# Down and output projections: the order of the three terms of a split product, high·high, low·high, high·low instead of high·high, high·low, low·high

## The reference

```python
x = x + mixer(rmsnorm(x, g1)) @ w_o            # output projection, 1024 x 1024
u = rmsnorm(x, g2) @ w_up                      # 1024 x 5632
g, v = split(causal_conv3(u))
x = x + (silu(g) * v) @ w_down                 # down projection, 2816 x 1024
```

## Time and profile before

| | us |
|---|---|
| median of 3 runs | 1048.58 |
| lowest, highest | 1048.35, 1048.67 |
| the profiled execution | 1048.49 |
| its span, first to last instruction | 1046.7 |
| TensorE matmul busy | 1041.2 |
| TensorE weight loads busy | 972.2 |
| VectorE, ScalarE, GpSimd busy | 866.1, 687.8, 348.1 |

### The profile page before, as it was taken

How to read it: one execution, slowest core, us unless ns; L and a number is a source line. 1 busy time by engine, 2 the same in 40 slices (tenths; PEclk the granted TensorE clock), 3 DMA queues, 4 the chain that set the end, 5 groups by cost and what they waited for, 6 DMA issues and landing times.

```text
span 1046.7 us, 21191 instructions
## 1 busy us (share of the span) xinstructions
PE 1041.2 (99%) x7496; PEld 972.2 (93%) x7496; DVE 866.1 (83%) x1589; ACT 687.8 (66%) x1264; POOL 348.1 (33%) x370
## 2 busy tenths in 40 slices
PE   9999999999999999999999999999999999999998
PEld 8999999999999999999989899999998998999998
DVE  7877778777799988887776999888896769998886
ACT  7766776766766656576776766655686766665662
POOL 5312222122355333322121564333350025543332
PEclk9999999999999999999999999999999999999999
DMA  9654555455466555535453666565434436665541
GB/s 321 226 162 152 159 159 171 147 174 203 160 217 212 196 195 188 173 107 181 144 180 121 202 210 208 184 191 192 145 107 144 152 119 215 213 198 192 190 157 41
DMA packets 57749, 183.34 MB, mean 175 GB/s; under 512 B 6352, under 2 KB 9680, under 8 KB 57424
## 3 DMA queue, kind: packets, MB, share of 16 engines
q1 hardware_dynamic: 56816, 181.52, 53.6%
q10 hardware_dynamic: 864, 0.92, 0.3%
HBM read 181.36 MB, written 1.05 MB: 174 GB/s over the span
## 4 chain that ended last, share of the span: by engine, by line
PE 94%; DVE 5%; DMA 0%; issue 0%; ACT 0%; DVEq 0%
PE ps L417 20%; PE ps L419 10%; PE ps L665 10%; PE ps L667 9%; PE ps L666 9%; PE ps L1747 6%; PE ps L1749 6%; PE ps L1748 6%; DVE w_lo L385 2%; PE ps L1223 2%; PE ps L1224 2%; PE ps L1225 2%; PE ps L599 1%; PE ps L843 1%; PE ps L888 1%; PE ps L817 1%
## 5 line engine op out<-in xcount | busy, mean ns | idle before, releaser
L385 DVE TENSOR_TENSOR w_lo<-w_raw,w_hi 128x1024 fp32r<-128x1024 f32 (+2 forms) x369 | 443.6, 1217 | 41.6 <-ACT w_hi L377 41.3
L377 ACT ACTIVATE w_hi<-w_raw 128x1024 fp32r<-128x1024 f32 (+2 forms) x369 | 353.8, 972 | 141.7 <-PE ps L419 119.0
L417 PE MATMUL ps<-xg,w_hi 128*128 128x512 f32 x1056 | 364.4, 391 | 0.0
L419 PE MATMUL ps<-xg,w_lo 128*128 128x256 f32 x1056 | 292.0, 277 | 0.0
L417 PEld LDWEIGHTS ps<-xg,w_hi 128*128 128x128 f32 x1056 | 198.3, 188 | 40.0 <-DVE xg L482 0.4
L419 PEld LDWEIGHTS ps<-xg,w_lo 128*128 128x128 f32 x1056 | 198.2, 188 | 0.1
L1869 POOL TENSOR_TENSOR prob_t<-prob_t,qkT 128x256 f32<-128x256 f32 x63 | 102.8, 1632 | 274.8 <-ACT prob_t L1792 274.8
L665 PE MATMUL ps<-w_hi,xg 128*128 128x384 f32 (+1 forms) x556 | 192.6, 346 | 0.0
L667 PE MATMUL ps<-w_hi,xg 128*128 128x384 f32 (+1 forms) x556 | 187.3, 337 | 0.0
L666 PE MATMUL ps<-w_lo,xg 128*128 128x384 f32 (+1 forms) x556 | 186.1, 335 | 0.0
L1749 PE MATMUL ps<-g_hi,w_lo 128*128 128x256 f32 x528 | 148.7, 282 | 0.0
(11 more groups left out here) (191 smaller groups left out, 1386.5 us busy)
## 6 DMA issues: line engine op xcount, KB each, us to landing
w_raw<-w_stream SPq DMA_DIRECT2D x228, 512.0 KB, 3.8
w_raw<-w_stream SPq DMA_DIRECT2D x137, 384.0 KB, 3.4
w_raw<-w_stream SPq DMA_DIRECT2D x4, 392.0 KB, 3.1
con<-consts SPq DMA_DIRECT2D x1, 1024.0 KB, 7.7
x_all<-x_t SPq DMA_DIRECT2D x4, 256.0 KB, 4.6
conv_taps<-taps SPq DMA_DIRECT2D x1, 1024.0 KB, 8.1
w_raw<-w_stream SPq DMA_DIRECT2D x4, 192.0 KB, 4.5
x_all<-x_a SPq DMA_DIRECT2D x3, 256.0 KB, 5.6
```

Of the source, the lines that this page charges most:

```text
L377: nc.scalar.activation(w_hi[s][:, 0:w], w_raw[s][:, 0:w], ACT.Copy).then_inc(w_hi_done, 1)
L385: nc.vector.tensor_tensor(w_lo[s][:, 0:w], w_raw[s][:, 0:w], w_hi[s][:, 0:w].bitcast(F32), ALU.subtract).then_inc(w_lo_done, 1)
L417: nc.tensor.matmul(bank(b, 0, 2 * TOK), w_hi[s][:, k * P:(k + 1) * P], xg[e][:, k, :, :].rearrange("p h t -> p (h t)"), start=(k == 0), st ...
L419: last = nc.tensor.matmul(bank(b), w_lo[s][:, k * P:(k + 1) * P], xg_hi[e][:, k, :], start=False, stop=(k == KT - 1), skip_group_check=True)
```

## The change

The second and third matmul of each triple change places. Nothing else is touched: the same 2160 matmuls (528 triples in the down projections, 192 in the output projections) run with the same operands and write to the same places. The stationary operand was high, high, low and becomes high, low, high; the moving one was high, low, high and becomes high, high, low. The semaphores stay on the last matmul of the triple.

```diff
@@ out_pe
             wh, wl = w_hi[s][:, m * P:(m + 1) * P], w_lo[s][:, m * P:(m + 1) * P]
             nc.tensor.matmul(out_acc(m), wh, mix_hi[st][:, k, :], start=(idx == 0 and m % 2 == 0), stop=False, skip_group_check=True)
-            nc.tensor.matmul(out_acc(m), wh, mix_lo[st][:, k, :], start=False, stop=False, skip_group_check=True)
-            last = nc.tensor.matmul(out_acc(m), wl, mix_hi[st][:, k, :], start=False, stop=(idx == KT - 1), skip_group_check=True)
+            nc.tensor.matmul(out_acc(m), wl, mix_hi[st][:, k, :], start=False, stop=False, skip_group_check=True)
+            last = nc.tensor.matmul(out_acc(m), wh, mix_lo[st][:, k, :], start=False, stop=(idx == KT - 1), skip_group_check=True)
@@ ffn_pe
                     nc.tensor.matmul(acc(m), wh, g_hi[f][b], start=first, stop=False, skip_group_check=True)
-                    nc.tensor.matmul(acc(m), wh, g_lo[f][b], start=False, stop=False, skip_group_check=True)
-                    last = nc.tensor.matmul(acc(m), wl, g_hi[f][b], start=False, stop=True, skip_group_check=True)
+                    nc.tensor.matmul(acc(m), wl, g_hi[f][b], start=False, stop=False, skip_group_check=True)
+                    last = nc.tensor.matmul(acc(m), wh, g_lo[f][b], start=False, stop=True, skip_group_check=True)
```

## The result

The changed kernel takes 1053.66 us (median of 5 runs, 1053.37 to 1053.76) against 1048.59 us for the kernel before, measured beside it: a ratio of 1.0043, 95% interval 1.0032 to 1.0054. It is slower by 5.1 us, and the profiled span grew by as much, from 1046.7 to 1051.8 us. Forecast were 1048.7 us, in 1045.5 to 1051.6.

What follows compares the result with a forecast made beforehand. TensorE, busy for 99% of the span, was taken as the bound. Terms (a) to (d) summed as 0 + 0 + 0.1 + 0 = +0.1 us, giving 1048.7 us on the median, in a range of 1045.5 to 1051.6.

Steps and rivals of the forecast that it cites:

- (d), the seams: Entry to and exit from the triples: sequence begun and left one place later, bounds +-1.3 us, taken as 0.
- the neighbouring up projection falls into its slow rhythm: Slower: up projection pairs 10 ns longer, 2.9 us per FFN (1051.5 from one); chance 0.16, with worse triples.
- (a), the reload: Second matmul of a triple, old order: its reload is neither skipped nor short, so the extra weight change costs 0.
- (b), the rate in steady flow: Triples in steady flow: rate set by operand positions modulo 256 bytes and nothing finer, so 0 for 656 triples.
- (c), the output projection of C: 64 triples whose parts start at 192 and 64: taken as +0.1 us, between -0.8 and +1.1 us.
- The faster rival: Down and output projections gain from alternating loads as in the up projection: full price -3.7 us, 1044.9; chance 0.14.
- The cheap reload: Triples: old order had a cheap reload of the same weights, new one pays 7.9 us, 1056.5; chance 0.03.

Runs made afterwards that it cites:

- `last_old`: Changed kernel with the eighth and last triple of every down projection back in the old order: 1048.2 us, ratio 0.9994.
- `last_new`: Kernel before with only the eighth and last triple of every down projection in the new order: 1053.84 us, ratio 1.0051.
- `end_hh`: Kernel before, last triple of every down projection as high weights by low activations, low by high, high by high: 1053.81 us, ratio 1.0051.
- `before_again`: Kernel before, unchanged, looked at once more in one execution: 1048.97 us.
- `new_g8`: Changed kernel with the gated activations of all three FFNs at FFN A's position (192 modulo 256 bytes): 1046.84 us, ratio 0.9988.
- `old_g8`: Kernel before with the gated activations of all three FFNs at FFN A's position (192 modulo 256 bytes): 1046.92 us, ratio 0.9987.
- `new_g0`: Changed kernel with the gated activations of all three FFNs at FFN B's position (160 modulo 256 bytes): 1055.05 us, ratio 1.0058.

## Why the prediction was wrong

**The step that failed is (d), the seams.** I bounded a seam by what the first triple of a down projection costs, 15 ns each and 1.3 us in all, and took 0. That is the entry into the down projection. The exit decides the rhythm of the 16 pairs behind it: 10 ns a pair, 160 ns a step, in two FFNs. The rival "the neighbouring up projection falls into its slow rhythm" named this mechanism, place and price per step, and shared a chance of 0.16 with worse triples; my argument against it, that "the sequence of positions is the same up to one place", was the error. At a seam that one place is the whole difference: a triple that ends in low weights (192) or in high ones (128), as `last_old`, `last_new` and `end_hh` show. The range took in one FFN in the long rhythm (1051.5); in the runs B and C fell together. Its price of 2.9 us per FFN was close: 2.58 and 2.44 us, lower since B and C had paid 15 and 22 ns per step before, in two first pairs that were late. The trace before already showed that the way out of a down projection depends on the position; in FFN B, the first L417 behind the seam and the next two:

```profile
643.15 0.39 PE L417 MATMUL ps<-xg,w_hi 128*128 128x512 f32 x1
...
643.50 0.40 PE L417 MATMUL ps<-xg,w_hi 128*128 128x512 f32 x1
...
643.85 0.39 PE L417 MATMUL ps<-xg,w_hi 128*128 128x512 f32 x1
```

These two pairs take 0.70 us where two take 0.68 in steady flow. The other argument against the rival, that runs within 0.3 us leave the rhythm no chance, held for the steps behind the first down projections; ahead of them `before_again` differs from the first profile.

**(a), the reload, was right.** Loads stay at 188 ns in the changed lines, their count is unchanged, and with low and high weights at one position the two orders agree to 0.3 us.

**(b), the rate in steady flow, was right in the main.** The totals of the down projections changed by 0.00, -0.33 and +0.17 us. In FFN A and in `new_g8` against `old_g8` they are the same to 0.01 us. That the position sets the rate is borne out by `new_g0` (down projections of C from 63.30 to 62.03 us) and `new_g8`. The runs move operands by 32 or 64 bytes and never by 128 or 256, so they don't show with what period the position counts. The small changes in B and C show that the order does act there, which (b) put at nothing: worked out from the traces, a down projection in the loop takes 2838 ns before and 2820 after in B, and 2871 and 2880 in C. The 109 ns that (b) set beside its rows come from a formula that the page "TensorE: Matmul & The Clock Gate" of the Trainium skill (section "Back-to-back issue gap") gives for an isolated matmul, while for a stream of loads and matmuls it gives other figures, none of them for 256 columns.

**(c), the output projection of C, was right.** It was put at +0.1 us, and the three output projections together took 70.40 us in both traces.

**The faster rival** (alternation is what makes the up projection quick) is out: with the whole of the new order and no seam in the way, `new_g8`, the down projections run at the old order's rate. **The cheap reload** is out with (a).

What stays open is the mechanism below the rule: why this neighbour at this position leads into the one rhythm or the other. No experiment looked at that, and the rule is shown for the three positions 160, 192 and 224 alone. Since `xg` starts at 192 in all runs, it isn't shown either whether 192 is safe by itself or because the two moving operands at the seam then start at the same place. `G_AT` moves the operand of all 24 matmuls, so its place in the last one alone wasn't tried.

## What to carry to other kernels

When TensorE is the bound, the distance between matmul starts is the thing to read, line by line and stage by stage, and a change of order must be costed for the code behind it as well: the end of one loop can set the pace of the next one, here through all 32 matmuls of a step, in 17 or 18 steps of a stage. Before giving up such an order, move the operands: here one tuple of SBUF offsets made the order indifferent and the kernel 0.12% quicker than the one before. A mean over all of a line's instances blurs this (394 ns against 391); min/median/max within one stage shows it at once.

## What the runs showed of the hardware that was not expected

- One instruction stream on the same addresses has two stable rhythms, 340 and 350 ns for a pair of 512 and 256 columns at a granted clock of 1.00, and, but for the first one or two pairs, stays in either for a whole stretch of 32 matmuls.
- Which one follows, from step 5 of an FFN on, depends on where the last stationary tile ahead of it starts (128 with one at 192 before it, or 192; modulo 256 bytes) together with where its moving operand starts: 192 leads into the short rhythm with both (`new_g8`, `old_g8`), 160 and 224 with the latter only (389 ns in `before`, 395 in `after`). This is shown with the low weights at 192 and the up projection's own operands at their places.
- Moving the low weights by 64 bytes, to the same position as the high ones, cost 11 us (1.0%), at an unchanged number of instructions and bytes. The Trainium skill, page "TensorE: Matmul & The Clock Gate", section "Step-by-step: what each phase is for", says that loading the next weights takes no SBUF bandwidth from the running matmul; whatever the cause, here a pair of load and matmul does depend on where both operands lie.
